# The start of the feed-forward stage: three units multiplied in step behind the second norm, the fourth in its own place, and block combinations shared between GpSimd and VectorE

## The reference

```python
x = x + gt_a * rmsnorm_2(mix @ w_out, g_post_attn)          # "x3" below
h = rmsnorm_2(x, g_pre_ffn) * (1.0 + sc_f) + sh_f
f = (silu(h @ w_gate) * (h @ w_up)) @ w_down                # w_gate, w_up: 2048 x 5632
x = x + gt_f * rmsnorm_2(f, g_post_ffn)
```

## Time and profile before

| | |
|---|---|
| median of 3 runs | 3037.09 us (3036.88 to 3038.49) |
| span of the profiled execution, first to last instruction | 3035.4 us; its own time stands nowhere beside it |
| TensorE busy | 3011.8 us, 99% of the span |
| VectorE, ScalarE, GpSimd busy | 2268.8, 1243.8, 362.1 us |
| TensorE's granted clock, mean | 0.998 |

### The profile page before, as it was taken

The page is one execution under the profiler, slowest core; times in us unless marked ns, Lnnn a source line. Parts: engine busy times, 40 slices in busy tenths (PEclk is TensorE's granted clock), DMA queues, the critical chain, the costliest instruction groups (busy, mean ns, idle before and its releaser), DMA issues.

```text
span 3035.4 us, 41372 instructions
## 1 busy us (share of the span) xinstructions
PE 3011.8 (99%) x15348; PEld 2530.7 (83%) x15348; DVE 2268.8 (75%) x2837; ACT 1243.8 (41%) x1593; POOL 362.1 (12%) x524
## 2 busy tenths in 40 slices
PE   8999999999999999999999999999999999999998
PEld 7888887888888888888888788888888888888887
DVE  6766646868887666777765788888888888888875
ACT  5223352213234333444442454444444444344433
POOL 0211100111110111001000200000000000011123
PEclk9999999999999999999999999999999999999999
DMA  5444353876765444344342256666666666588774
GB/s 189 140 133 136 123 205 118 325 274 219 269 232 198 167 166 166 123 162 165 126 153 97 111 177 180 176 176 179 174 172 171 169 175 180 184 228 228 228 227 160
DMA packets 120797, 544.95 MB, mean 180 GB/s; under 512 B 22304, under 2 KB 22576, under 8 KB 80880
## 3 DMA queue, kind: packets, MB, share of 16 engines
q1 hardware_dynamic: 63856, 321.15, 29.9%
q0 software_dynamic: 53232, 195.38, 23.3%
q10 hardware_dynamic: 3600, 26.98, 2.3%
HBM read 434.13 MB, written 37.76 MB: 155 GB/s over the span
## 4 chain that ended last, share of the span: by engine, by line
PE 98%; DVE 2%; DMA 0%; ACT 0%; issue 0%; DVEq 0%; ACTq 0%
PE PS L1983 18%; PE PS L1539 16%; PE PS L1541 15%; PE PS L1540 15%; PE PS L1986 9%; PE PS L2053 3%; PE PS L2052 3%; PE PS L2050 3%; PE PS L2018 1%; PE PS L2019 1%; PE PS L2020 1%; PE PS L1852 1%; PE PS L1592 1%; PE PS L1594 1%; PE PS L1593 1%; PE PS L1840 1%
## 5 line engine op out<-in xcount | busy, mean ns | idle before, releaser
L1539 PE MATMUL PS<-XHL,WH 128*128 128x512 f32 x1952 | 765.5, 392 | 0.3 <-DVE BB L2550 0.2
L1541 PE MATMUL PS<-XHL,WL 128*128 128x512 f32 x1952 | 760.0, 389 | 0.0
L1540 PE MATMUL PS<-XHL,WH 128*128 128x512 f32 x1952 | 759.6, 389 | 0.0
L982 ACT ACTIVATE WH<-RAW 128x2048 fp32r<-128x2048 f32 x137 | 262.0, 1913 | 475.1 <-PE PS L1541 472.4
L1539 PEld LDWEIGHTS PS<-XHL,WH 128*128 128x128 f32 x1952 | 366.4, 188 | 82.6 <-issue 5.7
L1541 PEld LDWEIGHTS PS<-XHL,WL 128*128 128x128 f32 x1952 | 366.4, 188 | 76.9
L1540 PEld LDWEIGHTS PS<-XHL,WH 128*128 128x128 f32 x1952 | 366.5, 188 | 75.0 <-issue 0.2
L2069 DVE TENSOR_TENSOR WL<-RAW,WH 128x2048 fp32r<-128x2048 f32 x136 | 311.0, 2287 | 86.4 <-ACT WH L982 86.3
L1327 ACT ACTIVATE QH<-RAW 128x1024 fp32r<-128x1024 f32 x210 | 222.1, 1059 | 250.0 <-PE PS L1986 237.2
L1983 PE MATMUL PS<-XHL,QH 128*128 128x512 f32 x1008 | 316.5, 395 | 0.0
L2923 DVE TENSOR_TENSOR QL<-RAW,QH 128x1024 fp32r<-128x1024 f32 x210 | 256.4, 1222 | 59.4 <-ACT QH L1327 59.4
(11 more groups left out here) (442 smaller groups left out, 5271.3 us busy)
## 6 DMA issues: line engine op xcount, KB each, us to landing
RAW<-w_units_dram SPq DMA_DIRECT2D x228, 1024.0 KB, 4.9
ADA<-w_ada_dram POOLq DMA_DIRECT2D x112, 512.0 KB, 5.6
ADAQ<-w_ada_dram POOLq DMA_DIRECT2D x80, 512.0 KB, 5.5
A<-w_units_dram SPq DMA_DIRECT2D x32, 1024.0 KB, 8.0
SUM<-RAW POOLq DMA_DIRECT2D x42, 512.0 KB, 4.6
RAW<-SUM POOLq DMA_DIRECT2D x42, 512.0 KB, 4.5
FRAW<-f_dram SPq DMA_DIRECT2D x4, 2048.0 KB, 13.0
A<-A POOLq DMA_DIRECT2D x8, 1024.0 KB, 7.5
```

Source lines behind the costliest of these rows:

```text
L982: act.activation(WH[:, slot, :], RAW[:, slot, :], ACT.Copy).then_inc(hi_ready, 1)
L1539: pe.matmul(PS[:, bank, :], wh, rh[:, x, :], start=k == 0, stop=False)
L1540: pe.matmul(PS[:, bank, :], wh, rl[:, x, :], start=False, stop=False)
L1541: ins = pe.matmul(PS[:, bank, :], wl, rh[:, x, :], start=False, stop=k == n - 1)
```

## The change

- TensorE multiplies three units in step: behind each tile of the second comes the same tile of the third (`product`, bank 2, weights in slot 1 of `WH`, `WL`). The fourth follows alone from `PAIRH`, `PAIRL`, once these are free in halves, into bank 5 (`UPBANK`).
- `XBANK` keeps three banks; VectorE waits for ScalarE's copy of the tile three before (`x_copied`).
- The third unit's weights are split by ScalarE ahead of the norm's last square root, and by VectorE in two halves (`home_lo`), one ahead of the tiles and one behind tile 3. The fourth's are split in halves: `fourth_hi` on ScalarE, `home_lo` on VectorE.
- `scaled_by_row` stands at other tiles (`SCALED_AT`). One weighted sum is folded into `ACCC` on VectorE, and a `token_sums` of TensorE goes. The second `clocked` has six matmuls, not four.
- Three of the four combinations go to GpSimd, tile by tile: 24 additions or subtractions of 128 x 256, the first eight between its additions to `BB`, sixteen behind. VectorE keeps one.
- SP stores `BB`, in five pieces, with the loads of the first fast pair between them. The second pair's loads wait for the fourth unit.
- The Silu table is loaded ahead of the tiles. ScalarE's and VectorE's lists behind the tiles are in another order. `rope_v`, `lam_v` and the like become counts of `prm_v`, `prm_a`.

```diff
-    XBANK = (2, 3, 4, 6)
+    XBANK = (3, 4, 6)
+    UPBANK = (1, 5)
...
+            def x3_save(t0, t1):
+                sp.wait_ge(x3_ready, t1)
+                sp.dma_start(x3_d[:, t0:t1, :], BB[:, t0:t1, :]).then_inc(x3_saved, 16)
+            x3_save(0, 4)
             for k in range(2):
+                if k == 1:
+                    for t0, t1 in ((4, 8), (8, 12), (12, 14), (14, 16)):
+                        x3_save(t0, t1)
                 sp.wait_ge(lo_ready, U_FFN + 3 + k)
                 sp.dma_start(RAWS[0][:, k, :], w_units[U_FFN + 2 * PLAIN + k]).then_inc(pair_loaded[0], 16)
-            sp.wait_ge(out_done, O_FFN + 2)
+            sp.wait_ge(out_done, O_FFN + 4)
...
                 gp.tensor_tensor(BB[:, t, :], BB[:, t, :], RES[:, t, :], ALU.add).then_inc(x3_ready, 1)
+                if t >= FULL_K:
+                    k = t - FULL_K
+                    gp.wait_ge(x_copied, k + 1)
+                    ins = gp.tensor_tensor(RES[:, k, LO], RES[:, k, LO], RES[:, k, HI], ALU.subtract)
+            ins.then_inc(t_sum, 1)
+            gp.drain()
+            gp.wait_ge(t_sum, 2)
+            for k in range(FULL_K):
+                gp.tensor_tensor(RES[:, FULL_K + k, HI], RES[:, FULL_K + k, HI], RES[:, k, LO], ALU.add)
+            gp.drain()
+            gp.wait_ge(t_lo, 1)
+            for k in range(FULL_K):
+                ins = gp.tensor_tensor(RES[:, k, LO], RES[:, FULL_K + k, LO], RES[:, FULL_K + k, HI], ALU.subtract)
+                if k % 4 == 3:
+                    ins.then_inc(t_sum, 1)
...
-            pair(U_FFN, O_FFN, X_FFN, True)
-            third(U_FFN + 2, O_FFN + 2, 3, 2, X_FFN)
-            unit(U_FFN + 3, 1, O_FFN + 3, [FULL], 3, 4, X_FFN)
+            for k in range(TILES + LAG):
+                if k < TILES:
+                    paired(0, k, U_FFN, X_FFN, own=True)
+                if k >= LAG:
+                    ins = paired(1, k - LAG, U_FFN, X_FFN, own=True)
+                    if k - LAG == TILES // 2 - 1:
+                        ins.then_inc(half_used, 1)
+                    if k == LAG:
+                        pe.wait_ge(half_lo, 5)
+                    if k - LAG == TILES // 2:
+                        pe.wait_ge(lo_ready, U_FFN + 3)
+                    ins = product(WH[:, 1, :], WL[:, 1, :], 2, k - LAG)
+            ins.then_inc(out_done, 1)
+            pe.wait_ge(half_lo, 6)
+            for k in range(TILES):
+                if k == TILES // 2:
+                    pe.wait_ge(lo_ready, U_FFN + 4)
+                ins = product(PAIRH, PAIRL, UPBANK[1], k)
```

More of the change, by code:

```diff
@@ L105 @@
 LAG = 1
+SCALED_AT = {1: (5, 7), 3: (7, 9), 6: (9, 11), 8: (11, 13), 10: (13, 16)}
+PRM_ROPE = 4
 U_LAST, O_LAST = U_QKV + 42, O_QKV + 42
@@ L405, in build @@
         sig_ready, sig_used, ple_loaded = sem("sig_ready"), sem("sig_used"), sem("ple_loaded")
-        saved, misc_loaded, rope_v, rope_a, lam_v, lam_a = (
-            sem(n) for n in ("saved", "misc_loaded", "rope_v", "rope_a", "lam_v", "lam_a"))
+        saved, misc_loaded = sem("saved"), sem("misc_loaded")
+        x_copied, x3_saved = sem("x_copied"), sem("x3_saved")
         rope_ready, vt_ready, vtr_done, vs_ready, qk_done = (
@@ L1450, in _ @@
             ins.then_inc(t_hi, 1)
+            plain_silu(0)
             plain_silu(1)
-            act.wait_ge(t_sum, 4)
+            act.wait_ge(pair_loaded[0], 32)
+            hi_part(0, 0, 0, 0, 1)
+            hi_part(0, 0, 1, 1, 1)
+            hi_part(0, 0, 2, 2, 1)
             for t in range(FULL_K):
+                if t % 4 == 0:
+                    act.wait_ge(t_sum, 3 + t // 4)
                 b = 3 * DT + FULL_K + t
@@ L1989, in fast_pair, with product @@
                     ins.then_inc(q_done, 1)
-            pair(U_FFN, O_FFN, X_FFN, True)
-            third(U_FFN + 2, O_FFN + 2, 3, 2, X_FFN)
-            unit(U_FFN + 3, 1, O_FFN + 3, [FULL], 3, 4, X_FFN)
+            def product(wh, wl, bank, x):
+                wh, wl = wh[:, x * P:(x + 1) * P], wl[:, x * P:(x + 1) * P]
+                pe.matmul(PS[:, bank, :], wh, XH[:, x, :], start=x == 0, stop=False, skip_group_check=True)
+                pe.matmul(PS[:, bank, :], wh, XL[:, x, :], start=False, stop=False, skip_group_check=True)
+                return pe.matmul(PS[:, bank, :], wl, XH[:, x, :], start=False, stop=x == TILES - 1,
+                                 skip_group_check=True)
+            for u in range(2):
+                pe.wait_ge(out_read, READ0 + O_FFN + u - 1)
+            for k in range(TILES + LAG):
[16 more added lines that the diff above has]
+                ins = product(PAIRH, PAIRL, UPBANK[1], k)
+            ins.then_inc(out_done, 1)
             with pe.Fori(0, LOOPED // 4) as i:
@@ L2859, in _ @@
                     modulation(V_GPF, 4 * DT)
+                    v.tensor_tensor(DS, MOD[:, 3 * DT:3 * DT + FULL_K], MOD[:, 3 * DT + FULL_K:4 * DT], ALU.subtract)
+            v.drain()
+            v.wait_ge(last_square, 1)
+            v.scalar_tensor_tensor(out=ACCC[:, :], in0=SIG[:, 1, :], scalar=G2[:, DT - 1:DT], in1=ACCC[:, :],
+                                   op0=ALU.mult, op1=ALU.add).then_inc(prod_ready, 1)
             v.wait_ge(out_read, READ0 + O_FFN)
@@ L2891, in _, with home_lo @@
             v.reciprocal(e, e).then_inc(scale_ready, 1)
-            scaled_by_row(5, 7)
+            def home_lo(hi, lo, raw, h, count):
+                part = slice(h * D // 2, (h + 1) * D // 2)
+                v.wait_ge(hi_ready if h or count is None else half_hi, U_FFN + 3 if count is None else count)
+                v.tensor_tensor(lo[:, part], raw[:, part], f32(hi[:, part]), ALU.subtract)\
+                 .then_inc(lo_ready if h else half_lo, 1)
+            home_lo(WH[:, 1, :], WL[:, 1, :], RAW[:, 0, :], 0, None)
             v.wait_ge(row_ready, 4)
@@ L3076, in _, with third_t @@
             ins.then_inc(t_lo, 1)
+            def third_t(tiles):
+                for t in tiles:
+                    m = 3 * DT + FULL_K + t
+                    ins = v.scalar_tensor_tensor(out=TC[:, t, hi], in0=RES[:, FULL_K + t, hi], scalar=MOD[:, m:m + 1],
+                                                 in1=f32(TC[:, t, lo]), op0=ALU.add, op1=ALU.subtract)
+                return ins
             sum_3(0, 32)
@@ L3080, in _ @@
             sum_1(0)
+            lo_part(0, 0, 2, 2)
+            plain_hidden(0)
             plain_hidden(1)
             v.drain().then_inc(copied, 1)
-            lo_part(0, 0, 2, 2)
             lo_part(0, 0, 3, 3)
             v.wait_ge(t_hi, 3)
-            for t in range(FULL_K):
-                m = 3 * DT + FULL_K + t
-                ins = v.scalar_tensor_tensor(out=TC[:, t, hi], in0=RES[:, FULL_K + t, hi], scalar=MOD[:, m:m + 1],
-                                             in1=f32(TC[:, t, lo]), op0=ALU.add, op1=ALU.subtract)
-            ins.then_inc(t_lo, 1)
+            third_t(range(FULL_K)).then_inc(t_lo, 1)
             lo_part(0, 0, 4, 0)
```

101 lines of the change are left out of this document (48 added, 53 removed).

## The result

The changed kernel took 3040.27 us in the median of 20 runs (3039.86 to 3044.80), the kernel before 3036.36 us beside it (20 runs, 3035.95 to 3038.49 and one of 3328.50): ratio 1.0015, 95% interval 1.0009 to 1.0021. The ratio lies under the bound of 0.2%, so the class is "no difference"; the interval leaves out 1, so a small loss is measured, 3.9 us by the medians. Forecast were 3039.8 us and a loss of 2.7. The profiled span is 3039.0 us, 3.6 longer. Its times read 0.25 us less than those of the profile before for the same work at the norm (a ScalarE row at 1711.80 is at 1711.55 now). Where the text compares them with times of before or of the prediction, it puts both on one scale and says which.

The account below looks back on a forecast made before the run. TensorE, busy 99% of the span, was taken as the bound. Reaching the fast pairs 4.0 us earlier, against product waits of 2.1, 2.3, 1.6, 0.6 and 0.1, gave +2.7: median 3039.8 us, range 3036.0 to 3044.5.

Parts of the forecast that it names:

- Start and three in step: Units start 0.9 us earlier, three units share each tile with one 1.4 us wait; TensorE reaches the fast pairs 4.0 earlier.
- The rest is mostly the clock: First four units before the change: of 4.6 us lost, 1.8 are waits, and half-rate clock cost 1.7.
- the fall that I allowed for at the first tile: Clock may drop after the early idle 1.4 us: third unit 1.5 us later, 0.8 of it swallowed by later waits.
- The small instruction: GpSimd's combinations of 256 elements behind the tiles: 0.69 us each, bounds 0.64 and 1.275.
- the prediction's own second sum: The whole change recomputed with 0.74 us per small GpSimd instruction, from the skill's figure: +3.3 us.
- The later products: First fast pair: products 3 to 6 wait 2.3, 1.6, 0.6 and 0.1 us for the lists of VectorE and ScalarE.
- the 6 to 7 that were to show it: Sign in the first fast pair: TensorE waits 6 to 7 us for `QL`, and none in the second.
- What costs nothing: Bank waits, table load, early GpSimd subtractions, moved stores, later second-pair loads and merged semaphores add no time.
- 3 us to spare: Margin of the adding DMA, put at 5.4 us, beside the second pair's loads behind the fourth unit.
- A: Behind the tiles, GpSimd and VectorE don't hold each other up: sum -0.8 us, or +0.7 if the clock falls; chance 0.15.
- B: At the fast pairs, the whole 4.0 us is kept because weights land earlier and lists keep pace: 3033.1; chance 0.04.
- C: Behind the tiles, each engine holds the port to its very end: +6.0 us, second form +12.4; chance 0.17.

Follow-up runs that it names:

- e4: The kernel before with sixteen added idle GpSimd memsets of 512 elements, and VectorE made to wait for their end: 3036.28 us.
- e12: The changed kernel with the first fast pair's two adding DMAs cut to 128 of 1024 columns, leaving that work out: 3040.12 us.
- e3: The kernel before with sixteen added idle GpSimd additions of 256 elements, and VectorE made to wait for their end: 3044.27 us.
- e1: The changed kernel with GpSimd's sixteen late combinations given back to VectorE as two instructions of 2048 elements: 3036.46 us.
- e2: As e1, but ScalarE's copies of `TC` stand ahead of the first weight operands, as in the kernel before: 3037.37 us.
- e5: The changed kernel with the third unit alone behind the first two instead of in step with them: 3043.51 us.
- e11: As e2, but the first fast pair's two adding DMAs add only 128 of 1024 columns, leaving that work out: 3033.22 us.

## Why the prediction was right, point by point

The class (no difference), the sign and the mechanism hold: TensorE comes earlier, and the lists behind the tiles, lengthened by the shared port, take back more than that. The sum was 1.1 us short (+2.7 against +3.8 in the trace). That 3039.8 came within 0.5 us of 3040.27 is in part luck: it was counted from the profiled execution of before plus 1.7, some 0.7 above the later median of 3036.36.

- **Start and three in step.** Right. With 0.25 added, the units start at 1723.3 (forecast 1723.6), the one wait is 1.43 (1.4), the third ends at 1757.9 (1757.7), the fourth at 1768.8 (1768.6). TensorE comes 3.86 earlier (4.0). The second weight lands at 1764.9 (1765.0).
- **The clock.** Wrong twice. "The rest is mostly the clock", said of the 4.6 us lost before, was read off one execution: in e4, with the same code there and no fall, TensorE waits 4.7 for `XL` instead of 3.5 and needs 48.21 us from its first matmul (1723.31) to the first fast product (1771.52), against 48.16. VectorE's pace sets it, and the slow clock only filled the waits. And the fall that I allowed for at the first tile came behind the 3.07 us instead. It cost nothing more: product 3's operand is ready at 1782.3, and without the 1.66 TensorE would have waited that much longer for it. In e12, with the same wait, it cost 1.68.
- **The small instruction.** The mis-sized term. "(1.275 - 0.10) / 2 + 0.10 = 0.69": measured 0.739 beside the tiles. With 0.74 less 0.2, a meeting costs VectorE 0.54, and 0.52 to 0.55 is what e3 shows. With 0.25 added, GpSimd's sixteen end at 1770.8, not 1768.5. `TA` is done 0.5 later than forecast, and `sum_3` and `QL`, each held by 0.5, take 3.4 together where the forecast had 2.7: the first `QL` is done at 1771.9, not 1770.7. Those 1.2 us are the 1.1 short. The 0.05 alone does not make them: the prediction's own second sum, with the 0.74 that it had estimated from the page "GPSIMD Engine Reference" of the Trainium skill, was +3.3. The row agrees with that 0.74. The other 0.5 us lie in `sum_3` and `QL`, held longer than the schedule had them; no run separates the two parts.
- **The later products.** Forecast 2.3, 1.6, 0.6, 0.1 for products 3 to 6; measured 0.60 behind 1.66 of clock (2.26 together), 1.52, 0.55, 0.09. For the same reason the waits for `QL` are 5.1 us in all and not the 6 to 7 that were to show it. Right: from `TC` on the lists hold them, as e1 shows, which has the port free and the waits at 3, 4 and 5 still.
- **What costs nothing.** Right for this kernel (e12), and the "3 us to spare" for the adding DMA were there (landed 1778.4, wanted by ScalarE's `QH` 4 at 1781.38). But the forecast took that margin for granted: it is there only because `QL` is so late that the loads are mostly done when the DMA starts. In e1, e2 and e5 it takes 10.7 to 12.2.
- **The rivals.** A (no mutual hold) falls with e3. B (all of the 4.0 kept) would have needed the lists, the port and the transfers cured at once; e11 is nearest to it, with part of the work left out. C (held to the very end) would make `QL` 1.96 long and the first product 1774.0 (measured 1.74 and 1772.0). The words "for the whole instruction", which the prediction took from the Trainium skill, "SBUF — State Buffer", "Who interferes with whom", stand there at VectorE's two-port modes; what the section says of all cases is an exclusive lock, and the 0.52 to 0.55 us of a 0.74 us instruction are less than that. A's sum of -0.8 is what e1 tests in part: 0.0.

Not tried: a layout in which the second pair's loads don't lie over the fourth unit's home, so that they could leave earlier; no kernel run here that does all of the work beats the one before.
